# One decoder step's expert layer: pairs overlapped on TensorE, outputs scattered to (choice, token) rows, unused slots left out by a bound

## The reference

```python
lg = t @ w_rg + b_rg                       # 4 groups; the best one, oh_g, with weight p_top
le_sel = einsum('tge,tg->te', einsum('td,gde->tge', t, w_re) + b_re, oh_g)
top_v, top_i = top_k(le_sel, 2)            # two of the group's 8 experts
w2 = softmax(top_v) * p_top
hid = silu(t @ w_eg[e]) * (t @ w_eu[e])    # for each chosen expert e
y = sum over the two choices of w2 * (hid @ w_ed[e])
```

## Time and profile before

| | us |
|---|---|
| device time, median of 3 runs (lowest, highest) | 1275.48 (1272.78, 1286.4) |
| span of the profiled execution | 1275.2 |
| first pair's gate/up product starts | 970.17 |
| last pair's down product ends | 1238.18 |

### The profile page before, as it was taken

One profiled execution on the slowest core, in us unless ns is written; L12 is line 12 of the kernel. 1 busy time (PEld: TensorE's weight loads), 2 busy tenths in 40 slices (PEclk: granted clock), 3 DMA queues, 4 the chain that ended last, 5 costly groups with the idle time before them and its releaser, 6 DMA issues. The chain is left out here.

```text
span 1275.2 us, 15545 instructions
## 1 busy us (share of the span) xinstructions
PE 969.1 (76%) x5808; PEld 686.8 (54%) x5808; DVE 545.3 (43%) x879; ACT 351.6 (28%) x615; POOL 119.5 (9%) x142
## 2 busy tenths in 40 slices
PE   3999998777667778497979767769636888888860
PEld 3888887655445555385758666448532333333320
DVE  3574712435665444342645562453263222232224
ACT  4453222001663323333455343233300000000000
POOL 1350000313000000000112300000101000000003
PEclk9999999555698978798979888889766999998885
DMA  7111214201407999762340040783354999999946
GB/s 227 67 67 66 79 54 141 66 5 26 132 22 229 293 261 293 231 256 79 114 150 1 33 166 31 266 298 131 96 205 145 416 422 422 423 422 422 423 196 224
DMA packets 80979, 242.22 MB, mean 190 GB/s; under 512 B 21280, under 2 KB 21920, under 8 KB 66464
## 3 DMA queue, kind: packets, MB, share of 16 engines
q1 hardware_dynamic: 72848, 219.34, 47.7%
q0 software_dynamic: 3616, 13.11, 2.8%
q10 hardware_dynamic: 4464, 9.08, 1.8%
HBM read 218.04 MB, written 23.46 MB: 189 GB/s over the span
## 5 line engine op out<-in xcount | busy, mean ns | idle before, releaser
L1917 PE MATMUL bank<-gate_up,slot_rows_t 128*64 128x512 f32 x512 | 114.9, 600 | 1.5 <-DVE slot_rows_t L1958 0.9
L349 PE MATMUL bank<-in_wh,in_hth 128*128 128x512 f32 x224 | 88.5, 395 | 3.1 <-DVE in_wl L293 3.1
L1934 PE MATMUL bank<-down,hidden_t 128*64 128x512 f32 x256 | 81.9, 798 | 8.3 <-issue 7.3
L350 PE MATMUL bank<-in_wl,in_hth 128*128 128x512 f32 x224 | 87.9, 393 | 0.0
L351 PE MATMUL bank<-in_wh,in_htl 128*128 128x512 f32 x224 | 87.9, 392 | 0.0
L1917 PEld LDWEIGHTS bank<-gate_up,slot_rows_t 128*64 128x64 f32 x512 | 42.7, 139 | 70.8 <-issue 70.8
L1123 PE MATMUL bank<-ident,k_half 128*128 128x128 f32 x320 | 54.0, 319 | 18.4 <-DVE window_k_t L1025 8.2
L1123 PEld LDWEIGHTS bank<-ident,k_half 128*128 128x128 f32 x320 | 41.3, 162 | 30.9 <-DVE window_k_t L1025 15.9
L1934 PEld LDWEIGHTS bank<-down,hidden_t 128*64 128x64 f32 x256 | 26.8, 178 | 52.3 <-issue 52.3
L1964 DVE TENSOR_SCALAR swish<-swish 128x256 f32<-128x256 f32 x16 | 4.7, 294 | 108.8 <-ACT swish L1942 108.8
L349 PEld LDWEIGHTS bank<-in_wh,in_hth 128*128 128x128 f32 x224 | 42.6, 190 | 12.3 <-issue 3.5
(11 more groups left out here) (376 smaller groups left out, 2133.5 us busy)
## 6 DMA issues: line engine op xcount, KB each, us to landing
gate_up<-w_exp_gate SPq DMA_DIRECT2D x32, 1024.0 KB
gate_up<-w_exp_up SPq DMA_DIRECT2D x32, 1024.0 KB
down<-w_exp_down SPq DMA_DIRECT2D x32, 1024.0 KB
in_w<-w_in SPq DMA_DIRECT2D x7, 2048.0 KB, 8.0
k_half<-cache_win_k SPq DMA_DIRECT2D x48, 256.0 KB, 7.1
v_half<-cache_win_v SPq DMA_DIRECT2D x48, 256.0 KB, 5.3
k_half<-cache_win_k SPq DMA_DIRECT2D x8, 1024.0 KB, 10.8
v_half<-cache_win_v SPq DMA_DIRECT2D x8, 1024.0 KB, 9.7
```

The source lines that it names most:

```text
L349: pe.matmul(o, hi, wh[b % 2][:, c, :], start=(c == 0), stop=False)
L350: pe.matmul(o, hi, wl[b % 2][:, c, :], start=False, stop=False)
L1917: last = pe.matmul(m.bank[2][64 * h:64 * h + 64, :], B.xt[s][:, c, 64 * h:64 * h + 64], B.gu[s][h][:, :, c, :], start=(c == 0), stop=(c == ...
L1934: last = pe.matmul(m.bank[4 + j][64 * h:64 * h + 64, :], B.hidt[s][:, k, 64 * h:64 * h + 64], B.dn[s][h][:, k, 512 * j:512 * j + 512], sta ...
```

## The change

One block takes the place of three.

- POOL's gathers carry a bound: `slot_token` is now the token, or 8191 for an unused slot, and rows beyond the bound are left out. Both row buffers are set to zero once in `route`.
- The outputs are scattered by POOL (L1917 of the changed kernel) straight to row (choice * 576 + token), with a bound for unused slots; ACT's direct stores are gone. A second index, `slot_out_row`, is made by ten more matmuls. `place` and the nine zero tiles are gone.
- The last additions read plain rows: SP loads ten tiles after the last scatter has landed.
- PE's order is one pair deeper: gate and up of pair k+1, turn the rows of pair k+2, then hidden and down of pair k. Gate/up has two PSUM banks. The loops are written out.
- Every engine loads the overflow count at the block's start.

```diff
@@ route
+            for s in range(2):
+                pool.memset(m.experts.rows[s][:], 0.0).then_inc(cleared, 1)
@@ route, PE, behind the ten matmuls of slot_token
+            pe.wait_ge(oh_done, 3)
+            for k in range(2):
+                for t in range(NT):
+                    last = pe.matmul(m.bank[3][:, 0:NPW], sa[:, k, t, :], pbo[:, k, t, :], ...)
+            last.then_inc(ix_done, 1)
@@ route, DVE
-            link(dve.scalar_tensor_tensor(q, tau, float(SLOT), r, ALU.mult, ALU.add))
-            link(dve.tensor_copy(m.place[:], q))
+            dve.tensor_tensor(pbo[:], ph[:], over(C("out_row")...), ALU.mult).then_inc(oh_done, 1)
...
             dve.wait_ge(ix_done, 1)
-            link(dve.tensor_copy(m.idx[:], m.bank[2][:, 0:NPT]))
+            link(dve.tensor_scalar(spare, at, 0.0, C("dump"), ALU.is_equal, ALU.mult))
+            link(dve.scalar_tensor_tensor(m.idx[:], at, -1.0, spare, ALU.add, ALU.add))
+            dve.wait_ge(ix_done, 2)
+            # the same two for m.out_row, from m.bank[3]
@@ experts
+    def gather(pool, n, dst, sem):
+        pool.indirect_dma_start(dst, None, m.rows_dram, bass.IndirectOffsetOnAxis(m.idx[:, n:n + 1], 0),
+                                bounds_check=T - 1, oob_is_err=False).then_inc(sem, 16)
+    def scatter(pool, n, src, sem):
+        pool.indirect_dma_start(y_rows, bass.IndirectOffsetOnAxis(m.out_row[:, n:n + 1], 0), src, None,
+                                bounds_check=2 * T - 1, oob_is_err=False).then_inc(sem, 16)
+        def _(sp):
+            for k in range(2, NPAIR):
+                sp.wait_ge(gu_done, k - 1)
+                B.load_gate_up(sp, k % 2, ...)
+                sp.wait_ge(y_done, k - 1)
+                B.load_down(sp, k % 2, ...)
...
+            sp.wait_ge(y_out, 16 * NPAIR)
+            for t in range(NT):
+                for k in range(2):
+                    sp.dma_start(got[t][k][:r], y_rows[k * T + t * P:k * T + t * P + r, :]).then_inc(row_in[t], 16)
+        def _(pool):
+            gather(pool, 0, B.rows[0][:], r_in[0])
+            gather(pool, 1, B.rows[1][:], r_in[1])
+            for k in range(NPAIR):
+                if k + 2 < NPAIR:
+                    pool.wait_ge(xt_done, 2 * k + 2)
+                    gather(pool, k + 2, B.rows[k % 2][:], r_in[k % 2])
+                pool.wait_ge(y_ev, 2 * k + 2)
+                if k:
+                    pool.wait_ge(y_out, 16 * k)
+                scatter(pool, k, B.y[k % 2][:], y_out)
+        def _(pe):
+            turn_rows(0); gate_up(0); turn_rows(1)
+            for k in range(NPAIR):
+                if k < LAST:
+                    gate_up(k + 1)
+                if k + 2 < NPAIR:
+                    turn_rows(k + 2)
+                down(k)
+        def _(dve):
+            store_rows(0); store_rows(1); swish(0)
+            for k in range(NPAIR):
+                if k + 2 < NPAIR:
+                    store_rows(k + 2)
+                if k < LAST:
+                    swish(k + 1)
+                store_out(k)
```

More of the change, by code:

```diff
@@ L1198, in later @@
         m.w_mem.load(sp)
[L1199 to L1204, removed]
+    residual(nc, m, "wo", m.w_o, m.Z, later)
 def residual(nc, m, name, weights, rows_at, later, hooks={}):
@@ L1633, in route @@
     xs = m.at("moe_rows", m.HTH, [NT, D])
[L1634 to L1635 removed]
+    cst = m.at("route_const", m.WH + 6720, [NCONST])
+    wr = m.at("router_w", m.WH + 5040, [C8, NG + NE])
     tri = m.at("earlier", m.WH + 512, [P])
@@ new lines, in experts @@
+    y_rows = m.slots_dram
+    got = [[m.at(f"expert_rows{t}{k}", m.Z + 2048 * t + 1024 * k, [D]) for k in range(2)] for t in range(NT)]
+    S = lambda n: m.sem("ex_" + n)
+    r_in, y_out = [S("rows0_in"), S("rows1_in")], S("out_written")
+    xt_done, xt_ev, gu_done, ex_done, hid_done = S("rows_turned"), S("rows_t_stored"), S("gate_up"), S("exped"), S("hidden")
+    ht_done, ht_ev, y_done, y_ev, ch = S("hidden_turned"), S("hidden_t_stored"), S("down"), S("out_copied"), S("swish_chain")
+    four = lambda ap: ap.rearrange("p (c n) -> p c n", c=4)
@@ new lines, in experts @@
+    gu_bank = lambda n: m.bank[(2, 6)[n % 2]]
+    LAST = NPAIR - 1
+    V = lambda n: m.sem("ov_" + n)
+    v_gu_in, v_dn_in, v_r_in, v_y_out = V("gate_up_in"), V("down_in"), V("rows_in"), V("out_written")
+    v_xt_done, v_xt_ev, v_gu_done, v_ex_done, v_hid = V("rows_turned"), V("rows_t_stored"), V("gate_up"), V("exped"), V("hidden")
+    v_ht_done, v_ht_ev, v_y_done, v_y_ev, v_ch = V("hidden_turned"), V("hidden_t_stored"), V("down"), V("out_copied"), V("swish_chain")
+    row_in = [m.sem(f"co_rows{t}") for t in range(NT)]
@@ new lines, in experts, with count @@
+    added, stores = m.sem("co_added"), m.sem("co_stores")
+    def count(eng):
+        return eng.value_load(m.novp[0:1, 0:1], min_val=0, max_val=NOVP)
+    def gather(pool, n, dst, sem):
[4 more added lines that the diff above has]
+                                bounds_check=2 * T - 1, oob_is_err=False).then_inc(sem, 16)
@@ new lines, in mm_turn, with mm_gate_up @@
+    def mm_turn(pe, s, j):
+        xr = B.rows[s][:].rearrange("p (d c) -> p d c", c=C8)
+        for c in range(4):
+            last = pe.transpose(m.bank[j][:, c * P:(c + 1) * P], xr[:, :, 4 * j + c], m.ident[:, :])
+        return last
+    def mm_gate_up(pe, s, bank):
+        for c in range(C8):
+            for h in range(2):
+                last = pe.matmul(bank[64 * h:64 * h + 64, :], B.xt[s][:, c, 64 * h:64 * h + 64],
+                                 B.gu[s][h][:, :, c, :], start=(c == 0), stop=(c == C8 - 1), skip_group_check=True)
+        return last
@@ new lines, in mm_turn_hidden, with mm_down @@
+    def mm_turn_hidden(pe, s):
+        for k in range(2):
+            last = pe.transpose(m.bank[3][:, k * P:(k + 1) * P],
+                                B.hid[s][:].rearrange("p (f k) -> p f k", k=2)[:, :, k], m.ident[:, :])
+        return last
+    def mm_down(pe, s):
+        for j in range(2):
+            for k in range(2):
+                for h in range(2):
+                    last = pe.matmul(m.bank[4 + j][64 * h:64 * h + 64, :], B.hidt[s][:, k, 64 * h:64 * h + 64],
+                                     B.dn[s][h][:, k, 512 * j:512 * j + 512], start=(k == 0), stop=(k == 1),
+                                     skip_group_check=True)
+        return last
@@ L2120, in combine @@
-def combine(nc, m, a):
-    got = [[m.at(f"expert_rows{t}{k}", m.Z + 2048 * t + 1024 * k, [D]) for k in range(2)] for t in range(NT)]
-    arrived, added, stores = [m.sem(f"co_rows{t}") for t in range(NT)], m.sem("co_added"), m.sem("co_stores")
-    with nc.Block() as block:
-        @block.gpsimd
-        def _(pool):
+            with sp.Else():
+                pass
+            sp.wait_ge(y_out, 16 * NPAIR)
             for t in range(NT):
@@ L2152, in _ @@
             sp.wait_ge(stores, 16 * NT)
+        @block.gpsimd
+        def _(pool):
+            n = count(pool)
+            gather(pool, 0, B.rows[0][:], r_in[0])
[8 more added lines that the diff above has]
+                scatter(pool, k, B.y[k % 2][:], y_out)
+            with pool.If(n > 0):
+                pool.wait_ge(xt_done, 2 * NPAIR)
+                pool.wait_ge(y_out, 16 * NPAIR)
+                for j in range(NOVP):
+                    with pool.If(n > j):
+                        if j:
+                            pool.wait_ge(v_xt_done, 2 * j)
+                        gather(pool, NPAIR + j, B.rows[0][:], v_r_in)
+                        pool.wait_ge(v_y_ev, 2 * j + 2)
+                        scatter(pool, NPAIR + j, B.y[0][:], v_y_out)
+                        pool.wait_ge(v_y_out, 16 * j + 16)
+                    with pool.Else():
+                        pass
+            with pool.Else():
+                pass
@@ L2269, in constants @@
     put("valid", tok < T)
-    put("token", tok * (tok < T))
+    put("token", (tok + 1) * (tok < T))
+    put("out_row", np.concatenate([(tok + k * T + 1) * (tok < T) for k in range(2)], axis=1))
+    put("dump", 8192)
     e = np.arange(NE)
```

405 lines of the change are left out of this document (179 added, 226 removed).

## The result

The changed kernel takes **1322.7 us** (median of 4, 1307.7 to 1329.6) against 1278.7 for the kernel before, timed beside it: ratio **1.031 [1.023, 1.038]**. The forecast was 1295, range 1263 to 1314. The direction is right, and the time lies above the range. The profiled execution's span is 1320.2, 45.0 longer than before.

A forecast was written before the change was run, and what follows sets the result against it. Transfers (17.4 us a pair) and PE's chain (17.1) were taken as limits side by side. Expert block +25.3, routing +2.5 and tail -8.2 gave +19.6 on the profiled 1275.2: 1295 us, range 1263 to 1314.

The forecast's parts named there:

- The ring: Expert block: each down product waits for a gather queued behind the previous down product's scatter; period 19.5 us.
- D: The end of one down product on PE in the expert block; the gather was to start 2.29 us later.
- L: Time from a gather's start to its landing in the expert block, taken as 9.7 us.
- low end: Rows thinned evenly over the DMA engines: L 8.0 us, with 0.9 for the scatter; as a rival 1273 us, chance 0.25.
- From D to the gather: On POOL: scatter starts 1.05 us after D, takes 0.94, gather follows 0.30 later; 2.29 in all.
- Turn to D: On PE, from the gather's landing: row turn 1.16 us, then 6.37 from hidden turn to end of down; 7.53.
- The first D: Start of the expert block: the first down product was to end 23.7 us after the first gate/up start.
- the last gate/up and two downs: End of the expert block: gate/up 7.09 us and two downs of 4.5 each, 16.1 together.
- Routing: Ahead of the expert block: index complete about 2.0 us later, then overflow count load 0.51 before the first gather; +2.5.
- Tail: From the last D to the end: 28.8 us for 37.0 before, -8.2; ends -10 with no waiting and -4.4.
- The rival that came nearest: Expert block: busiest DMA engine keeps all its rows, or unused rows are moved; L 11.4, 1317 us, chance 0.18.
- The other side: Expert block: the gather comes in time, L below 6.8 us, transfers decide, period 16.6; 1257 us, chance 0.12.

The follow-up runs named there:

- e1: Changed kernel, but POOL issues the gather of pair k+3 ahead of the scatter of pair k: 1280.5 us, ratio 1.001.
- e2: Changed kernel, but PE turns the rows of pair k+2 behind the down product of pair k: 1266.8 us, ratio 0.993.
- e6: Changed kernel with PE, DVE and ACT in the order of the kernel before; scatter on POOL and bound stay: 1262.6 us, ratio 0.993.
- e11: Changed kernel with every slot's index over the bound, so gathers move no row but keep 128 slots: 1305.3 us (one execution).
- e7: Changed kernel, but POOL issues the gather of pair k+2 right ahead of the scatter of pair k-1: 1280.9 us, ratio 1.009.
- e4: Changed kernel, but unused slots gather token 0, so every gather moves 128 rows: 1326.1 us, ratio 1.042.
- e3: Changed kernel with the used slots spread over the partitions, same rows and bytes moved: 1312.1 us, ratio 1.026.
- e8: Changed kernel with each weight load split into two, 4 KB per partition for 8 KB: 1305.1 us, ratio 1.028.
- e12: Changed kernel with each gather listing 16 slots instead of 128, all moved: 1305.6 us (one execution).
- e9: e2, and SP starts the gate/up weights of pair k+1 ahead of its wait for the down product: 1255.5 us, ratio 0.987.

## Why the prediction was wrong in size

- **The ring: right.** D to gather to turn to D is the path, PE stands idle at the turn, and e1, e2 and e6 each remove the loss by opening it. PE idles 7.1 us in each of the 13 periods where about 5 were named.
- **The failed step: L**, taken as 9.7, the middle of 8.0 and 11.4. Measured 11.1: 1.4 too little, 13 times, 18.6 us. The low end thinned the load's 3.8 us by the share of used rows (0.56). e11 shows that rows are the small part: with none at all it still takes 10.3. A left-out slot stays a packet and, by the records above, takes its turn among the weights; so the lone gather should not have been thinned below the 8.8 of the earlier trace rows, and the scatter adds 1.7 to it (e7), where the low end had 0.9.
- **From D to the gather: 2.85** for 2.29. The copies end 0.7 after D, as before within 0.1, but POOL starts the scatter 0.8 behind them (0.53 of it without a named cause), where ACT's store had followed after 0.2; the scatter takes 1.01 for 0.94. 0.56 x 13 = 7.3 us. Why POOL is slower off the mark was not tried. Turn to D is 7.64 for 7.53, 1.4 us, and there two misses cancel: the turn, behind 7 us of idle PE, takes 1.97 (at a granted clock of 0.50 in the period shown) where the 1.16 of a busy PE was taken, and the rest 5.67 for 6.37.
- The first D comes 24.6 after the first gate/up start (23.7 foreseen), the last gate/up and two downs take 16.1, as foreseen. The block is thus 24.6 + 13 x 21.62 + 16.1 = 321.8, +53.8 for +25.3.
- **Routing +2.3** (+2.5 foreseen), near by luck: the first gather starts 3.3 later, not 2.5, and lands 1.0 sooner, where nothing was counted. Its DMA engines are idle and it has fewer rows; with 128 rows it lands after 4.9 (e4), with the used ones after 4.0.
- **Tail 25.9** (28.8 foreseen, 37.0 before): the last scatter lands 2.6 after its start, not 5.0, and the additions wait 0.32, not 2.5. -11.1 for -8.2, past the better end of -10. e6 gives it a second time, 27.4 from the last D to the end; with a block only 1.4 shorter than before, its ratio of 0.993 is mostly the tail's.
- Sum: 53.8 + 2.3 - 11.1 = +45.0; the spans differ by 45.0.
- **The rival that came nearest** (1317) had the number and neither of its reasons: POOL's bytes say that rows are left out, and spreading the slots gave 0.3 us (e3). That its L of 11.4 came so near the 11.1 is partly luck: an engine's "full share" holds of packets, not of rows. The Trainium skill (DMA: Bandwidth & Descriptors, Queues, rings and completion order) states that a DMA engine goes round its queues and drains a whole packet of one before it switches; its packet is typically 9 to 17 descriptors, and whether a packet record of the trace is such a packet no run shows. The counts above, not far from one for one, agree with queues taking turns, and so does the sooner landing with smaller packets of weights (e8) and with fewer slots (e12 beside e11). No run here shows in what order an engine took them.
- The other side, L of 6.8 or less, did not come near: even 16 slots take 9.0 us, 3.1 to the first packet and 5.4 for the packets of scatter and gather. What stays **unexplained is the first packet**: beside weights it starts 4.1 us (before) to 4.7 us (e8) after its transfer's start, on idle engines after 2.0 (the first gather) or 1.5 (the last scatter).
- **A reading without effect:** the prediction has the DMA engines full in only one stretch; the earlier trace rows has three more nines, from about 414 to 510 us. The change does not act there, and nothing hung on it.

## What to carry to other kernels

Before an order is deepened on one engine, follow every queue that feeds it round to where it starts: here a gather stood behind a scatter, the scatter needed a down product, and on PE that product stood behind the turn of the rows of the gather before. One exchanged pair of steps on either engine was worth over 40 us. A bound on an indirect transfer saves bytes, not packets; where small packets share the engines with large ones, count the slots and not only the rows. And if a loop waits for its transfers, look at what their issuing queue waits for before looking at bytes: that order was worth the 12.8 us of block between e2 and e9.

## What the runs showed of the hardware

- On idle DMA engines rows decide how long a gather of 128 slots takes: the shortest landing was 2.1 with none moved (e11), 3.9 with the used ones (changed), 5.0 with all. Among 8 KB packets of weights they hardly do: 10.3, 11.1 and 11.5 on average from the gather's start to the turn (e11, changed, e4), and 9.0 for 16 slots, all moved.
- 144 packets of 4 bytes start within 0.2 us on idle engines; among weights the 288 of scatter and gather take 6.7 us, though three quarters of them have 4 bytes (e11).
- Splitting the weights' packets from 8 KB to 4 KB made gathers land 1.7 us sooner, but in that kernel PE also waited 19.8 us for gate/up weights, which it had not before.
